# Hybrid decoder trunk: retention first, RWKV second, and a new memory layout for the mixer

## The reference, cut to what matters

```python
p = x @ lp['w_in']
p_rw, p_ret, p_ml = _split(p, [RW_P, RET_P, ML_P])
p_rw_prev = _shift_prev(p_rw, st['rw_shift'] @ lp['w_in'][:, :RW_P])
mixed = p_rw + (p_rw_prev - p_rw) * lp['rw_mu']
...
mix = jnp.concatenate([o_rw, o_ret, o_ml], -1).astype(x.dtype) @ lp['w_out']
x1 = _layernorm(ALPHA * x + mix, lp['ln1_g'], lp['ln1_b'])
hdn = jax.nn.silu(x1 @ lp['w_gate']) * (x1 @ lp['w_up'])
x2 = _layernorm(ALPHA * x1 + hdn @ lp['w_down'], lp['ln2_g'], lp['ln2_b'])
```

## Time and profile before

| what | value |
|---|---|
| median of 3 runs | 3157.72 us (3151.95 to 3161.5) |
| profiled execution, its own time | 3165.72 us |
| its span | 3163.9 us |
| PE busy | 2950.7 us, 93% |
| DVE busy | 1610.8 us, 51% |
| ACT busy | 1202.7 us, 38% |
| mean granted TensorE clock | 0.949 of 2.4 GHz |
| DMA | 445 MB, 141 GB/s |

### The profile page before, as it was taken

One profiled execution on the slowest core, in us unless ns is written; L12 is line 12 of the kernel. 1 busy time (PEld: TensorE's weight loads), 2 busy tenths in 40 slices (PEclk: granted clock), 3 DMA queues, 4 the chain that ended last, 5 costly groups with the idle time before them and its releaser, 6 DMA issues.

```text
span 3163.9 us, 54407 instructions
## 1 busy us (share of the span) xinstructions
PE 2950.7 (93%) x22745; PEld 2820.8 (89%) x22745; DVE 1610.8 (51%) x1539; ACT 1202.7 (38%) x1315; POOL 0.2 (0%) x4
## 2 busy tenths in 40 slices
PE   7989899986999999999899899998969999999996
PEld 6978798876999999999899787987869999999996
DVE  6565443535554555444555644545455455555443
ACT  4343232313544444333354431332244444443333
POOL 0000000000000000000000000000000000000000
PEclk9999898978999999999999998988789999999998
DMA  4532153416555555555544222542355555555551
GB/s 145 179 95 61 42 162 108 153 40 129 163 184 179 179 180 178 180 180 165 147 146 143 80 61 60 170 149 87 103 96 181 181 177 181 179 180 172 180 180 68
DMA packets 285572, 445.02 MB, mean 141 GB/s; under 512 B 52110, under 2 KB 82578, under 8 KB 285114
## 3 DMA queue, kind: packets, MB, share of 16 engines
q1 hardware_dynamic: 283820, 439.29, 45.8%
q10 hardware_dynamic: 1600, 3.48, 0.3%
HBM read 430.94 MB, written 11.78 MB: 140 GB/s over the span
## 4 chain that ended last, share of the span: by engine, by line
PE 85%; DVE 7%; ACT 4%; DMA 2%; issue 2%; ACTq 0%; DVEq 0%; SPq 0%
PE psum L576 19%; PE psum L578 18%; PE psum L577 18%; PE psum L599 5%; PE psum L601 5%; PE psum L600 5%; PE psum L751 2%; DMA w_raw<-in_w_gate 2%; PE psum L649 2%; DVE w_lo L1333 1%; PE psum L876 1%; PE psum L742 1%; ACT resid L1105 1%; PE psum L888 1%; ACT w_hi L1053 1%
## 5 line engine op out<-in xcount | busy, mean ns | idle before, releaser
L1042 ACT ACTIVATE w_hi<-w_raw 128x1024 fp32r<-128x1024 f32 x624 | 661.4, 1061 | 1096.3 <-PE psum L578 1007.1
L1324 DVE TENSOR_TENSOR w_lo<-w_raw,w_hi 128x1024 fp32r<-128x1024 f32 x528 | 644.9, 1225 | 721.9 <-ACT w_hi L1042 716.1
L576 PE MATMUL psum<-x_hi,w_lo 128*128 128x264 f32 (+1 forms) x3424 | 981.5, 287 | 24.1 <-DVE x_lo L1415 23.2
L577 PE MATMUL psum<-x_lo,w_hi 128*128 128x264 f32 (+1 forms) x3424 | 977.4, 285 | 0.0
L578 PE MATMUL psum<-x_hi,w_hi 128*128 128x264 f32 (+1 forms) x3424 | 976.9, 285 | 0.0
L576 PEld LDWEIGHTS psum<-x_hi,w_lo 128*128 128x128 f32 x3424 | 648.0, 189 | 26.3 <-issue 24.8
L578 PEld LDWEIGHTS psum<-x_hi,w_hi 128*128 128x128 f32 x3424 | 648.4, 189 | 0.0
L577 PEld LDWEIGHTS psum<-x_lo,w_hi 128*128 128x128 f32 x3424 | 648.0, 189 | 0.0
L1333 DVE TENSOR_TENSOR w_lo<-w_raw,w_hi 128x1024 fp32r<-128x1024 f32 x272 | 328.9, 1221 | 255.2 <-ACT w_hi L1053 134.6
L576 PE MATMUL psum<-h_hi,w_lo 128*128 128x264 f32 x1408 | 401.8, 285 | 7.3 <-issue 5.2
L577 PE MATMUL psum<-h_lo,w_hi 128*128 128x264 f32 x1408 | 403.0, 286 | 0.0
(11 more groups left out here) (366 smaller groups left out, 2912.1 us busy)
## 6 DMA issues: line engine op xcount, KB each, us to landing
w_raw<-in_w_in SPq DMA_DIRECT2D x192, 512.0 KB, 3.6
w_raw<-in_w_gate SPq DMA_DIRECT2D x176, 512.0 KB, 3.6
w_raw<-in_w_up SPq DMA_DIRECT2D x176, 512.0 KB, 4.5
w_raw<-in_w_down SPq DMA_DIRECT2D x176, 512.0 KB, 4.1
w_raw<-in_w_out SPq DMA_DIRECT2D x64, 512.0 KB, 4.8
w_raw<-in_w_in SPq DMA_DIRECT2D x16, 262.0 KB, 2.9
...
```

The source lines that it names most:

```text
L576: mm(out, w1, bh[:, k, 0:nt], start=(k == 0), stop=False)
L577: mm(out, w0, bl[:, k, 0:nt], start=False, stop=False)
L1042: A(wh[:, j, :, :], raw[:, j, :, :], ACT.Copy).then_inc(S.hi_ready, 1)
L1324: TT(wl[:, j, :, :], raw[:, j, :, :], wh[:, j, :, :].bitcast(F32), ALU.subtract).then_inc(S.lo_ready, 1)
```

## The change

Retention runs before RWKV. Groups 3 and 4 run in the open, groups 5, 6, 7, 0 and 1 behind retention, group 2, the tail and groups 8 to 11 behind RWKV; mLSTM stays behind the output product, whose first part now takes row slabs 2, 3, 4 before 0, 1, since retention's output is ready first.

```diff
-IN_GROUPS = 12
+TAIL = 12
+IN_ORDER = (3, 4, 5, 6, 7, 0, 1, 2, TAIL, 8, 9, 10, 11)
+OPEN, RET_FILL = 2, 5
+RW_FILL = IN_GROUPS - OPEN - RET_FILL
...
+    ret_steps = [('shift', 1), ('swap', 6), ('swap1', 6), ('turn0', 20), ('turn1', 2), ('score', 2), ('num0', 2), ('num1', 5),
+                 ('vt', 4), ('v0', 4), ('v1', 3), ('v2', 2), ('sy', 3), ('sumsq', 3), ('spread', 6), ('spread1', 4)]
+    rw_steps = [
+        [('in', 3), ('a', 2), ('g', 2), ('kk', 5), ('kks', 2), ('bonus', 4)] +
+        chunk_steps(0, (4, 1, 1, 1), (1,) * 6, (1,) * 6, (2, 2, 2)) +
+        chunk_steps(1, (3, 1, 1, 1), (1,) * 6, (1,) * 6, (2, 2, 2)) +
+        [('sa', 4), ('sv', 4), ('sy', 4), ('gn', 3), ('gnss', 4), ('gnsp', 4)],
+        [('in', 3), ('a', 2), ('g', 2), ('kk', 5), ('kks', 2), ('v', 19), ('bonus', 2)] +
+        chunk_steps(0, (3, 1, 1, 1), (1,) * 6, (0, 1, 0, 1, 0, 0), (1, 1, 2)) +
+        chunk_steps(1, (2, 1, 1, 1), (1,) * 6, (0, 1, 0, 1, 0, 0), (1, 1, 2)) +
+        [('sa', 3), ('sv', 3), ('sy', 4), ('gn', 3), ('gnss', 4), ('gnsp', 3)]]
...
+    ret_plan = plan(ret_steps, 16 * RET_FILL)
+    rw_plan = [plan(rw_steps[l], 16 * RW_FILL) for l in range(DEPTH)]
```

On SP, the rotary and decay tables go behind slab 7 and a wait for the whole of x, the LoRA weights and the small inputs behind slabs 9 to 12, retention's sample state behind 13 to 15. RWKV's sample state is loaded behind slabs 92 to 95 in layer 0 and 95 to 98 in layer 1 (after `rw_inverted`), and stored behind the first four output slabs:

```diff
+                    if i == 7:
                         sp.wait_ge(S.x_ready, 10 * l + 5)
+                        sp.dma_start(rrot[:, :, :].rearrange("p a b -> p (a b)"), a['c_rot']).then_inc(S.rdec_loaded, 16)
+                        sp.dma_start(rdec[:, :, :].rearrange("p a b -> p (a b)"), a['c_ret']).then_inc(S.rdec_loaded, 16)
...
+                    first = 95 if l else 92
+                    if i == first:
+                        sp.wait_ge(S.rw_inverted, 2 * NCH * (l + 1))
+                    if first <= i < first + 4:
+                        sp.dma_start(srw[:, i - first, :, :], rwi[i - first]).then_inc(S.rw_sample_loaded, 16)
```

On ACT, tanh and sigmoid of the LoRA inputs come before retention, ACT copies out all groups but the two open ones, and the exponentials move ahead of the next step:

```diff
                 last.then_inc(S.rw_ka_done, 1)
-                bg.to('bonus')
                 act.wait_ge(S.rw_cum, l + 1)
...
                 A(enam[:, :, :], namid[:, :, :], ACT.Exp).then_inc(S.rw_exps, 1)
+                if l:
+                    bg.to('v')
+                    act.wait_ge(S.rw_v, l)
+                    for b in range(4):
+                        last = A(vsg[:, b, :], ps[:, 4 + b, 0:T], ACT.Sigmoid, bias=col(l, 'rw_v0', b))
+                    last.then_inc(S.rw_v_taken, 1)
+                bg.to('bonus')
```

On DVE, `rw_mixed` goes: `p_rw` is mixed in place through a difference tile of four blocks, the receptance group (0) behind retention's last slabs, the key group (1) at the start of RWKV, the value group (2) just before the bonus:

```diff
+            def mix(l, b0, n, i):
+                p, d = px[:, b0:b0 + n, :], diff[:, 0:n, :]
+                if i == 0:
+                    own(TT(d[:, :, 1:SEQ], p[:, :, 0:SEQ - 1], p[:, :, 1:SEQ], ALU.subtract))
+                if i == 1:
+                    own(TS(d[:, :, 0:1], p[:, :, 0:1], -1.0, None, ALU.mult))
+                if i == 2:
+                    own(TT(d[:, :, SEQ:T], p[:, :, T:TW], p[:, :, SEQ:T], ALU.subtract))
+                if i == 3:
+                    own(TT(d, d, over(cols(l, 'rw_mu', RW_PB)[:, b0:b0 + n], T), ALU.mult))
+                if i == 4:
+                    own(TT(p[:, :, 0:T], p[:, :, 0:T], d, ALU.add))
...
+                bg = Parts(rw_plan[l], lambda i: lo1(s0 + 8 * (OPEN + RET_FILL) + RING + i))
+                dve.wait_ge(S.evacuated, g0 + OPEN + RET_FILL)
                 for i in range(5):
+                    mix(l, 4, 4, i)
...
                 then(TT(mx[:, 4:8, :], mx[:, 4:8, :], mx[:, 0:4, :], ALU.mult))
+                dve.wait_ge(S.evacuated, g0 + OPEN + RET_FILL + 1)
+                for i in range(5):
+                    mix(l, 8, 4, i)
```

More of the change, by code:

```diff
@@ L337, in slab0 @@
         n = l * LAYER_SLABS
-        for name, slabs in (('tail', TAIL_SLABS), ('in', IN_GROUPS * 8), ('out', 32), ('up', 16 * FF_GROUPS),
+        for name, slabs in (('in', IN_GROUPS * 8), ('out', 32), ('up', 16 * FF_GROUPS),
                             ('down', 4 * DOWN_SLABS)):
@@ L347, in group0 @@
         n = 1 + l * LAYER_GROUPS
-        for name, groups in (('tail', 1), ('in', IN_GROUPS), ('out', 8), ('up', 2 * FF_GROUPS), ('down', 4)):
+        for name, groups in (('in', IN_GROUPS), ('out', 8), ('up', 2 * FF_GROUPS), ('down', 4)):
             if name == part:
@@ L363, in plan, with chunk_steps @@
         return out
-    rw_steps = [('in', 4), ('a', 0), ('g', 1), ('v', 1), ('kk', 4), ('kks', 1), ('bonus', 5), ('tok0', 4),
[6 rows of a table removed]
-    ret_steps = [('swap', 6), ('swap1', 7), ('turn0', 8), ('turn1', 2), ('score', 1), ('num0', 2), ('num1', 5),
-                 ('vt', 3), ('v0', 4), ('v1', 2), ('v2', 0), ('sy', 2), ('sumsq', 2), ('spread', 6), ('spread1', 2)]
+    ret_steps = [('shift', 1), ('swap', 6), ('swap1', 6), ('turn0', 20), ('turn1', 2), ('score', 2), ('num0', 2), ('num1', 5),
+                 ('vt', 4), ('v0', 4), ('v1', 3), ('v2', 2), ('sy', 3), ('sumsq', 3), ('spread', 6), ('spread1', 4)]
+    def chunk_steps(c, before, x, y, after):
+        levels = [(f'{what}{c}.{lev}', n[lev]) for lev in range(6) for what, n in (('x', x), ('y', y))]
+        return [(f'{name}{c}', n) for name, n in zip(('tok', 'pairs', 'more', 'l'), before)] + levels + \
+               [(f'{name}{c}', n) for name, n in zip(('w', 'u', 'out'), after)]
+    rw_steps = [
[7 more added lines that the diff above has]
+        [('sa', 3), ('sv', 3), ('sy', 4), ('gn', 3), ('gnss', 4), ('gnsp', 3)]]
     ml_steps = [('rows', 9), ('spread_m', 4), ('spread_e', 2), ('turn0', 2), ('turn1', 1), ('score', 1), ('num0', 2),
@@ L1317, in _ @@
             dve.sem_inc(S.gated, 1)
-            v.memset(raw[:, :, :, :], 0.0).then_inc(S.raw_cleared, 1)
             def lo4(s0, slots=range(RING)):
@@ new lines, in _ @@
+                            dve.wait_ge(S.evacuated, g0 + g + 1)
+                        if g or i > 1:
+                            lo1(s0 + 8 * g + RING + i)
+                        if g and i < 5:
+                            mix(l, 12, 2, i)
+                        if g and i == 5:
+                            dve.sem_inc(S.rw_mix, 1)
+                bg = behind_ret(l)
+                then = (lambda ins: (own(ins), bg.step()))
+                bg.to('shift')
+                dve.wait_ge(S.rdec_loaded, 32 * (l + 1))
@@ new lines, in _ @@
+                then(TT(pret[:, 0:6, 0:T], pret[:, 0:6, 0:T], each(rrot[:, 0, :], AH), ALU.mult))
+                then(TT(pret[:, 0:6, 0:T], pret[:, 0:6, 0:T], rtmp[:, :, :], ALU.add))
+                then(TS(pret[:, 3:6, 0:T], pret[:, 3:6, 0:T], 0.125, None, ALU.mult))
+                for dst, b0, t0 in ((qs, 0, AH), (kw, AP_, AH + AP_)):
+                    for c in range(NCH):
+                        cs = slice(CH * c, CH * c + CH)
+                        last = TT(dst[:, :, cs], pret[:, b0:b0 + AP_, cs], rdec[:, t0:t0 + AP_, :], ALU.mult)
@@ L1581, in _ @@
+                last.then_inc(S.a_prepared, 1)
+                attention(l, False, 2 * l, bg)
+                bg = Parts(rw_plan[l], lambda i: lo1(s0 + 8 * (OPEN + RET_FILL) + RING + i))
+                then = (lambda ins: (own(ins), bg.step()))
+                dve.wait_ge(S.evacuated, g0 + OPEN + RET_FILL)
                 for i in range(5):
-                    mix(3, i)
-                dve.sem_inc(S.rw_mix, 1)
-                dve.wait_ge(S.shift_turned, l + 1)
-                then(v.tensor_copy(pret[:, 0:2, :], praw[:, 14:16, :]))
+                    mix(l, 4, 4, i)
```

538 lines of the change are left out of this document (263 added, 275 removed), and 6 rows, old and new, of the table rw_steps.

## The result

The changed kernel takes 3186.73 us (median of 4 runs, 3184.75 to 3202.72), the kernel before in the same series 3159.61 (3151.95 to 3165.4). The ratio is 1.0098, with a 95% interval of 1.0059 to 1.0138: slower, by 27 us by the medians, where +10 was forecast. The time lies inside the range; the size is wrong by a factor of nearly three.

What follows compares the result with a forecast made beforehand. TensorE was taken to bound nearly everything. Waits removed -35.5, added in RWKV +32 and in retention +19.6, clock -6 made +10 us, taking the median from 3157.7 to 3168; range 3122 to 3190.

Steps and rivals of the forecast that it cites:

- `spread1`: Retention, behind spread1: only three weight blocks are ready while DVE works without a w_lo; TensorE idle 4.8 us.
- block 64: Retention: the copy-out comes late behind ACT's square root, sigmoid and a w_hi; a wait of 3.9 us.
- block 48: Retention: ACT's small copy and a w_hi go ahead of the copy-out; a wait of 2.7 us.
- the first copy-out: RWKV: ACT copies the first group out only behind the exponentials; TensorE waits 3.6 us, in layer 1 3.5.
- the sample product: RWKV, layer 1: the last sample load goes behind slab 98; a wait of 5.2 us where 1.5 stood.
- the end: End of RWKV: four ready blocks (5.8 us) stand against 7.9; a wait of 2.1 us a layer.
- The bonus product: RWKV, layer 0: behind two tail blocks TensorE waits 2.9 us more for DVE's work.
- `tok`: RWKV, layer 0: behind four tail blocks TensorE waits for DVE's rw_eend, 7.8 us idle.
- mixing in place: RWKV's value group on DVE: 0 to 4.35 us a layer, taken whole in layer 0, as nothing in layer 1.
- Net -6: TensorE's clock: 10.5 us regained in the RWKV stages, 4.5 in all lost to new waits.
- rival C: Each new wait above 3.5 us brings a 1.2 GHz stretch costing 2 to 3: 3194 us; chance 0.12.
- Rival B: Waits as forecast, but the clock returns wherever blocks stand between small matmuls, 22 for 6: 3152 us; chance 0.2.

Runs made afterwards that it cites:

- the other execution: In mLSTM's first step DVE splits the slabs before it waits for ACT's log of the forget gate, against the changed kernel: 3190.54 us.
- The made waits: Six waits of TensorE for DVE additions put on purpose into the open input slabs, against the changed kernel: 3211.01 us.

## Why the prediction was wrong

**The waits came where they were forecast, and their sum was 9 too high.** +16 of idle time was forecast for the input sections, and +7.1 came. Retention: +9.8 a layer forecast, to 14.9; 14.0 measured, with each of its waits within 0.3 (`spread1` 4.5 for 4.8, block 64 3.6 for 3.9, block 48 2.45 for 2.7). RWKV: 26 and 27 forecast, 23.0 and 24.8 measured. Here the first copy-out was 3.0 (3.6 and 3.5 forecast), the tail's 1.9 (2.0), the sample product 4.4 (5.2) and the end 1.9 (2.1). The bonus product waited 0.8 for 2.9 and `tok` 5.6 for 7.8, since mixing in place was counted whole as path, 4.35, and is 1.35 at `tok` and next to nothing in the section. Not forecast was 2.3 for `w_lo` behind `sa`.

**The step that failed is the clock: "Net -6".** The prediction took 10.5 us as regained and "only some, 4.5 in all" as new, because the earlier trace rows show a stretch where TensorE was idle a third of the time at 2.4 GHz. These are the waits of that stretch, in the kernel before:

```profile
PE psum L839 <- DVE rw_eend L1637: 2.5, 1, 2.5
PE psum L854 <- ACT rw_tok L1223: 1.5, 1, 1.5
```

It could say nothing of a single one of 3.6 or 4.5. The sections' busy time rose by 12.9 in the pair of traces, 19 us away from the forecast (by 5.8 with the other execution's, still 12 away), and the median missed by 17. The account, in the forecast's terms: 10 forecast, 9 less idle time and 19 more busy time in the input sections, 1 less in the rest, and 8 for the place of the profiled executions make the 27. Part of the agreement of the total with the range is luck, then: two errors of opposite sign. In layer 0 both drops that were to go, at 174 and 376, went; in layer 1 the one behind the sample product stayed, since the wait there grew to 4.4. The new ones behind waits of 1.9 and more outnumber them. That is rival C's mechanism, at a lower limit than the 3.5 it named. The price was 1.5 to 1.7 where it was measured by itself and 2.7 behind the 4.5 us wait of retention, where C named 2 to 3. Rival C's 3194 overshot because its waits were 9 too high and no drop of the kernel before was to go. Rival B, the clock recovering fully, is excluded by the rows. The Trainium skill's page "TensorE: Matmul & The Clock Gate" (HAM oscillation) says that idle gaps between bursts bring the half clock back. The made waits agree: the half clock stands behind the five of 2.3 us and more, though not behind the one of 1.9. The prediction had weighed that rule and set it aside for gaps this short.

**The section behind was left out.** The table loads made the mLSTM wait 2.7 longer in each layer. The prediction looked at DVE's start there (the stores) and not at the table with which ACT arrives.

**What stays open.** In the output section busy time lay between 156 and 173 us over the executions, 163.4 and 163.5 before; curing its first wait did not lower it. What decides whether a wait of 1.9 to 2.5 us has a half-clock stretch behind it was not found: the same wait had one in some executions and none in others, and in front of `tok`, with small matmuls behind them, the 2.5 of the kernel before and even the 3.4 of the run without the value mix had none. Nor was it found what brings the half-clock stretches that no wait precedes. How much of the 27 us is clock is bounded, not measured: the busy time of the input sections rose by 5.8 or 12.9, by which execution is taken. Whether the memory layout costs anything by itself wasn't tried.
